# VectorE empties bank 7 (GEMM halves, spatial gating) ahead of the next units' maxima in the first block's attention

## The chip, the cores and the metric

The kernel runs on one core of one Trainium2 chip. The metric is the device time of one execution in microseconds. The engines are TensorE (PE, with its weight loads as PEld), VectorE (DVE), ScalarE (ACT), GpSimd (POOL) and SyncE (SP). Each runs its own list of instructions in order, and they meet through semaphores.

## The reference, cut to what matters

Two blocks follow each other. The first has two layers, each with a projection, a mixer and a feed-forward part; the change is in the mixer. Of that the parts below matter here: three attention branches over 512 positions and 8 heads, and a spatial gating that is computed beside them.

```python
def first_block(x, ...):
    for l in range(DEPTH):                      # DEPTH = 2
        h = rmsnorm(x, attn_norm[l])
        (q, kc, vc, ksl, vsl, kwn, vwn, gts, gq, gk, gv, ga, gr, uv) = split_columns(h @ w_in[l])
        o_nsa = nsa_mixer(q, kc, vc, ksl, vsl, kwn, vwn, gts, ...)
        o_gla = gla_mixer(gq, gk, gv, ga, gr, ...)
        o_sg = spatial_gating(uv, ...)
        x = x + jnp.concatenate([o_nsa, o_gla.astype(x.dtype), o_sg], axis=-1) @ w_out[l]
        ...
def spatial_gating(uv, ln_g, ln_b, w_s, b_s):
    u, v = jnp.split(jax.nn.gelu(uv), 2, axis=-1)
    v = layernorm(v, ln_g, ln_b).reshape(B, nch, SG_CHUNK, SG_GROUPS, SG_CH)
    s = jnp.einsum('gij,bnjgc->bnigc', jnp.tril(w_s), v) + b_s.T[None, None, :, :, None]
    out = u.reshape(B, nch, SG_CHUNK, SG_GROUPS, SG_CH) * s
...
        s = jnp.einsum('bqghd,bkgd->bghqk', qb, kwb)      # in nsa_mixer, per block of queries
        p = masked_softmax(s, wmask[None, None, None])
        o_win = jnp.einsum('bghqk,bkgd->bqghd', p.astype(vwb.dtype), vwb)
```

## The kernel before, in words

Positions lie along the free axis of most tiles, channels on the 128 partitions. A GEMM of the first block takes 24 products of 128x512 into one of eight PSUM banks: eight slices, each as three products of high and low parts (lines 454, 457, 458).

The attention of a layer is cut into 32 units. A unit u is one pair of heads j, one block of 128 queries, and one branch: even units are the selected branch (there are 8 blocks of keys and up to 16 may be selected, so every earlier block is), odd units the window branch. A loop over v = 0 to 15 handles two units per turn; step is v modulo 4, and j is v divided by 4. Every engine has this loop written out in its own order, and there is no scheduler.

- **TensorE**, turn v: turn(2v), the transposes of the probabilities of unit 2v (line 706); the scores of units 2v+2 and 2v+3 (line 690, four banks, 0 to 3); turn(2v+1); the value products of units 2v-1 and 2v (line 742); then one extra piece of work, which uses bank 7. At step 0 it is turn_compressed, the transposes of the compressed branch's probabilities (line 726). At step 1 it is the next compressed scores (line 716). At steps 2 and 3 it is half of a GEMM, by the table HALVES: su1 at v = 2 and 3, gr0 at 6 and 7, gr1 at 10 and 11. At v = 13 and 14 it is the spatial gating (line 789, by GATING_AT).
- **VectorE**, turn v: the maxima of units 2v+2 and 2v+3 (line 1842, four reductions of masked scores, each with a read of its accumulator); the emptying of bank 7 if the turn before ended a GEMM (evict_half, line 1924) or a gating (gated, line 1931); scale(2v+2), a reciprocal and two multiplications (lines 1882 and 1887); at some steps work of the compressed branch; scale(2v+3); at some turns statistics for the gating (gating_stats) or low parts for the output GEMM (out_low, line 1918).
- **ScalarE**, turn v: turned_copy(2v) out of banks 4 and 5 (line 1304), the exponentials of unit 2v+2 (line 1282), turned_copy(2v+1), the exponentials of unit 2v+3, and at step 0 the copy of turned compressed probabilities (line 1295).

So the maxima of a unit release its exponentials, those release scale, and scale releases turn on TensorE in the next turn. Whoever fills bank 7 next waits until VectorE has emptied it. With the table, a GEMM ends in bank 7 at v = 3, 7 and 11, is emptied at v = 4, 8 and 12, and what waits for the bank there is turn_compressed. The first gating is emptied at v = 14, and the second one waits for it.

Of the kernel before, what the change touches and what calls it, by code (L numbers as in the profile page):

```python
# [122 lines left out]
def row_block(u):  # L123

    i = u // 2 % NT
    return i if u % 2 == 0 else NT - 1 - i
# [25 lines left out]
def build(nc, a_x, a_w, a_cmp, a_mod, a_c, a_const, a_misc, a_vec, a_rgw, a_rpb, a_out):  # L152
# [8 lines left out]
    with ctx:  # L161
# [117 lines left out]
        def m_(name):  # L279
            return misc[:, MISC[name][0]:MISC[name][1]]  # L280
# [119 lines left out]
        def filling(name):  # L400
            b, k = uses[name]
            return full[b], k + 1

        def emptying(name):
            b, k = uses[name]
            return free[b], k + 1
# [5 lines left out]
        def emptied(name):  # L412
            return free[uses[name][0]]
# [1149 lines left out]
        def _(dve):  # L1563
# [74 lines left out]
            for l in range(DEPTH):  # L1638
# [187 lines left out]
                U = HEADS * NT  # L1826
# [7 lines left out]
                def maxima(u):  # L1834
                    i, br = row_block(u), u % 2
                    w = (i + 1) * P
                    for hh in range(2):
                        dve.wait_ge(*filling((l, "S", hh, u)))
                    s2 = PS[:, 2 * br:2 * br + 2, :]
                    mask = before_diag[:, S - w:S]  # L1840
                    for hh in range(2):
                        V.tensor_tensor_reduce(s2[:, hh, 0:w], s2[:, hh, 0:w], mask, -1.0, -2 * NEG_MASK, ALU.add, ALU.min,  # L1842
                                               nmax[:, br, hh:hh + 1]).then_inc(max_ok.sem, 1)
                        dve.wait_ge(max_ok.sem, max_ok.raised())

                def compressed_masked(j):
                    dve.wait_ge(*filling((l, "Sc", j)))
                    sc = PS[:, 7, 0:NT * 64].rearrange("p (n h c) -> p n h c", h=2, c=32)[:, :, :, 0:NC]
                    pc = Pc[:, :, :, 0:NC]
                    if j:  # L1850
                        dve.wait_ge(*filling((l, "PTc", j - 1)))
                    TT(pc, sc, cm.unsqueeze(2).to_broadcast([P, NT, 2, NC]), ALU.add).then_inc(emptied((l, "Sc", j)), 1)
                    dve.wait_ge(*emptying((l, "Sc", j)))

                def compressed_distances(j):
                    pc = Pc[:, :, :, 0:NC]
                    V.tensor_reduce(maxc[:, :, :], pc, AX.X, ALU.max).then_inc(dve_chain.sem, 1)
                    dve.wait_ge(dve_chain.sem, dve_chain.raised())
                    TT(pc, pc, maxc[:, :, :].unsqueeze(3).to_broadcast([P, NT, 2, NC]), ALU.subtract)\
                        .then_inc(maxc_ok.sem, 1)  # L1860
                    dve.wait_ge(maxc_ok.sem, maxc_ok.raised())

                def scale_compressed(j):
                    pc = Pc[:, :, :, 0:NC]
                    dve.wait_ge(expc_ok.sem, expc_ok.seen_by("dve"))
                    V.tensor_reduce(sumsc[:, :, :], pc, AX.X, ALU.add).then_inc(dve_chain.sem, 1)
                    dve.wait_ge(dve_chain.sem, dve_chain.raised())
                    V.reciprocal(rc[:, :, :], sumsc[:, :, :]).then_inc(dve_chain.sem, 1)
                    dve.wait_ge(dve_chain.sem, dve_chain.raised())
                    both = 2 * j * BR + 2  # L1870
                    TT(rc[:, :, :], rc[:, :, :], gN[:, :, both:both + BR + 1:BR], ALU.mult).then_inc(dve_chain.sem, 1)
                    dve.wait_ge(dve_chain.sem, dve_chain.raised())
                    TT(pc, pc, rc[:, :, :].unsqueeze(3).to_broadcast([P, NT, 2, NC]), ALU.mult).then_inc(scaledc.sem, 1)
                    dve.wait_ge(scaledc.sem, scaledc.raised())

                def scale(u):
                    j, i, br = u // (2 * NT), row_block(u), u % 2
                    w = (i + 1) * P
                    both = 2 * j * BR + br
                    for hh in range(2):  # L1880
                        dve.wait_ge(*emptying((l, "S", hh, u)))
                    V.reciprocal(r3[:, 0:2], sums[:, br, 0:2]).then_inc(dve_chain.sem, 1)
                    dve.wait_ge(dve_chain.sem, dve_chain.raised())
                    for hh in range(2):
                        pr = work[:, 2 * br + hh, 0:w]
                        gate = gN[:, i, both + BR * hh:both + BR * hh + 1]
                        TS(pr, pr, r3[:, hh:hh + 1], gate, ALU.mult, ALU.mult).then_inc(scaled.sem, 1)  # L1887
                        dve.wait_ge(scaled.sem, scaled.raised())
# [5 lines left out]
                def gating_stats(n):  # L1894

                    if n == 0:
                        dve.wait_ge(*emptying((l, "sv1", "T")))
                    V.bn_stats(small[:, 8 + 6 * n:14 + 6 * n], sv[:, :, n, :]).then_inc(dve_chain.sem, 1)
                    dve.wait_ge(dve_chain.sem, dve_chain.raised())
                    V.bn_aggr(small[:, 32 + 2 * n:34 + 2 * n], small[:, 8 + 6 * n:14 + 6 * n]).then_inc(dve_chain.sem, 1)  # L1900
                    dve.wait_ge(dve_chain.sem, dve_chain.raised())
                    if n == NT - 1:
                        TS(small[:, 44:48], small[:, 33:40:2], EPS, None, ALU.add).then_inc(dve_chain.sem, 1)
                        dve.wait_ge(dve_chain.sem, dve_chain.raised())
                        TS(small[:, 40:44].bitcast(U32), small[:, 44:48].bitcast(U32), 1, None, ALU.logical_shift_right)                            .then_inc(dve_chain.sem, 1)
                        dve.wait_ge(dve_chain.sem, dve_chain.raised())
                        V.reciprocal(small[:, 48:52], small[:, 40:44]).then_inc(gating_ok.sem, 1)
                        dve.wait_ge(gating_ok.sem, gating_ok.raised())
# [6 lines left out]
                def out_low(k):  # L1915

                    dve.wait_ge(h_hi.sem, h_hi.seen_by("dve"))
                    TT(o_lo[k], mixed[k], o_hi[k].bitcast(F32), ALU.subtract).then_inc(h_lo.sem, 1)
                    dve.wait_ge(h_lo.sem, h_lo.raised())

                def evict_half(name):

                    dve.wait_ge(*filling((l, name)))
                    TT(proj[:, T[name], :], PS[:, 7, :], rstd[:, :], ALU.mult).then_inc(emptied((l, name)), 1)
                    dve.wait_ge(*emptying((l, name)))

                def gated(t):

                    key = (l, "sg", t)
                    dve.wait_ge(*filling(key))  # L1930
                    TT(sq[:, t, :].rearrange("p (n c) -> p n c", c=P), PS[:, 7, :].rearrange("p (n c) -> p n c", c=P),
                       m_("sgb")[:, t * P:(t + 1) * P].unsqueeze(1).to_broadcast([P, NT, P]), ALU.add)\
                        .then_inc(emptied(key), 1)
                    dve.wait_ge(*emptying(key))
# [9 lines left out]
                scale(1)  # L1944
                for v in range(U // 2):
                    j, step = v // NT, v % NT
                    for u in (2 * v + 2, 2 * v + 3):
                        if u < U:
                            maxima(u)
                    if v - 1 in HALVES and HALVES[v - 1][1] == 1:  # L1950
                        evict_half(HALVES[v - 1][0])
                    if v - 1 in GATING_AT:
                        gated(GATING_AT.index(v - 1))
                    if 2 * v + 2 < U:
                        scale(2 * v + 2)
                    if step == 2 and j + 1 < HEADS // 2:
                        compressed_distances(j + 1)
                    elif step == 3 and j + 1 < HEADS // 2:
                        scale_compressed(j + 1)
                    if 2 * v + 3 < U:  # L1960
                        scale(2 * v + 3)
                    if v in STATS_AT:
                        gating_stats(STATS_AT.index(v))
                    if v in CONVERT_AT:
                        out_low(CONVERT_AT.index(v))
                    if step == 1 and j + 1 < HEADS // 2:
                        compressed_masked(j + 1)
# [650 lines left out]
```

## Time and profile before

| | before |
|---|---|
| median of 3 runs | 1894.14 us (1894.01 to 1894.18) |
| the profiled execution | 1893.17 us, its span 1890.5 us |
| TensorE busy | 1835.7 us, 97% |
| GpSimd busy | 1530.4 us, 81% |
| VectorE busy | 1121.3 us, 59% |
| ScalarE busy | 659.7 us, 35% |

The two attention loops lie near 155 to 260 us and 795 to 900 us of the span. Shares are means over the whole span; in a window of the first loop, 145 to 265 us, TensorE was busy for 105.96, VectorE for 101.42 and ScalarE for 82.08 of 120 us.

### The profile page before, as it was taken

The page shows a single profiled execution, that of the slowest core. Times are in us where ns is not written, and L with a number is a line of the kernel's source. Part 1 is how long each engine was busy: PE and PEld are TensorE (multiplying, and loading weights), DVE is VectorE, ACT ScalarE, POOL GpSimd, SP SyncE. Part 2 cuts the span into 40 slices and gives each one's busy share as a digit, 9 for nine tenths or more (in the row PEclk, how much of TensorE's full clock was granted, in tenths as well). Part 3 has the DMA queues.
Part 4 walks back from the last instruction along what each step waited for, and adds up shares of the span by engine and source line. Part 5 has one row for each costly group of instructions (what it writes and reads, how often), then busy time and mean ns, then how long its engine had stood idle before and what let it go on. Part 6 is the DMA issues. An engine that isn't in the chain of part 4 may idle for free.

```text
span 1890.5 us, 28094 instructions
## 1 busy us (share of the span) xinstructions
PE 1835.7 (97%) x10354; PEld 1463.3 (77%) x10354; DVE 1121.3 (59%) x1627; ACT 659.7 (35%) x1146; POOL 1530.4 (81%) x1093
## 2 busy tenths in 40 slices
PE   8998899999999999988999999999999999999997
PEld 6776678888888877766888888888877777778885
DVE  4778865574366456888546415767846667650342
ACT  4356652110011232767321001123556665640112
POOL 8993569988888898715998878988799998689994
PEclk9999999999999999999999999999999999999999
DMA  5251023443344223300234333532223333323231
GB/s 200 79 162 40 13 68 110 135 132 101 100 134 123 89 79 104 120 13 24 89 102 145 121 95 106 153 116 77 89 84 87 97 85 93 83 77 101 89 100 45
DMA packets 68690, 182.53 MB, mean 97 GB/s; under 512 B 23888, under 2 KB 24144, under 8 KB 68432
## 3 DMA queue, kind: packets, MB, share of 16 engines
q1 hardware_dynamic: 60480, 154.48, 26.3%
q10 hardware_dynamic: 8080, 26.32, 4.4%
q8 instruction: 82, 1.34, 0.3%
q14 instruction: 48, 0.39, 0.1%
HBM read 178.67 MB, written 2.10 MB: 96 GB/s over the span
## 4 chain that ended last, share of the span: by engine, by line
PE 78%; DVE 8%; POOL 6%; issue 4%; ACT 3%; DMA 0%; SPq 0%; POOLq 0%; DVEq 0%; ACTq 0%
PE PS L454 23%; PE PS L458 23%; PE PS L457 23%; POOL w_lo L2325 3%; DVE work L1887 2%; POOL w_hi L2320 2%; POOL w_hi L2318 1%; PE PS L997 1%; DVE PS L1842 1%; ACT work L1282 1%; PE PS L690 1%; PE PS L586 1%; PE PS L918 1%; PE PS L955 1%; ACT work L1304 1%
## 5 line engine op out<-in xcount | busy, mean ns | idle before, releaser
L2325 POOL TENSOR_TENSOR w_lo<-raw,w_hi 128x256 fp32r<-128x256 f32 (+2 forms) x606 | 786.3, 1297 | 64.9 <-ACT w_hi L1389 16.8
L454 PE MATMUL PS<-a_hi,w_hi 128*128 128x512 f32 x1168 | 462.8, 396 | 5.6 <-POOL w_lo L2325 5.0
L458 PE MATMUL PS<-a_hi,w_lo 128*128 128x512 f32 x1168 | 455.5, 390 | 0.0
L457 PE MATMUL PS<-a_lo,w_hi 128*128 128x512 f32 x1168 | 455.5, 390 | 0.0
L2318 POOL TENSOR_SCALAR w_hi<-raw 128x512 fp32r<-128x512 f32 x226 | 372.4, 1648 | 100.8 <-PE PS L454 84.7
L2320 POOL TENSOR_TENSOR w_hi<-raw,const 128x1024 fp32r<-128x1024 f32 (+1 forms) x192 | 339.6, 1769 | 100.9 <-PE PS L454 95.2
L454 PEld LDWEIGHTS PS<-a_hi,w_hi 128*128 128x128 f32 x1168 | 219.5, 188 | 62.2 <-issue 8.4
L458 PEld LDWEIGHTS PS<-a_hi,w_lo 128*128 128x128 f32 x1168 | 219.7, 188 | 46.7
L457 PEld LDWEIGHTS PS<-a_lo,w_hi 128*128 128x128 f32 x1168 | 219.8, 188 | 44.7 <-issue 0.7
L454 PE MATMUL PS<-b_hi,w_hi 128*128 128x512 f32 x552 | 222.1, 402 | 3.4 <-ACT zs L1462 2.9
L457 PE MATMUL PS<-b_lo,w_hi 128*128 128x512 f32 x552 | 215.2, 390 | 0.0
L458 PE MATMUL PS<-b_hi,w_lo 128*128 128x512 f32 x552 | 214.8, 389 | 0.0
L2003 DVE TENSOR_TENSOR work<-PS,rstd 128x512 f32<-128x512 f32 x88 | 60.9, 692 | 148.5 <-PE PS L458 143.2
L1376 ACT ACTIVATE work<-work 128x512 f32<-128x512 f32 x44 | 27.8, 633 | 313.4 <-DVE small L2007 313.3
L454 PE MATMUL PS<-f_hi,w_hi 128*128 128x512 f32 x352 | 136.9, 389 | 0.0
L457 PE MATMUL PS<-f_lo,w_hi 128*128 128x512 f32 x352 | 136.9, 389 | 0.0
L458 PE MATMUL PS<-f_hi,w_lo 128*128 128x512 f32 x352 | 136.9, 389 | 0.0
L454 PEld LDWEIGHTS PS<-b_hi,w_hi 128*128 128x128 f32 x552 | 103.5, 188 | 33.1 <-issue 7.4
L458 PEld LDWEIGHTS PS<-b_hi,w_lo 128*128 128x128 f32 x552 | 103.7, 188 | 22.0
L457 PEld LDWEIGHTS PS<-b_lo,w_hi 128*128 128x128 f32 x552 | 103.7, 188 | 22.0 <-issue 1.9
L2014 DVE TENSOR_TENSOR f_lo<-work,f_hi 128x512 fp32r<-128x512 f32 x44 | 85.5, 1944 | 36.5 <-ACT f_hi L1379 36.5
L2061 DVE TENSOR_TENSOR x<-PS,x 128x512 f32<-128x512 f32 x32 | 22.1, 692 | 139.4 <-PE PS L458 139.2
(343 smaller groups left out, 2687.4 us busy)
## 6 DMA issues: line engine op xcount, KB each, us to landing
raw<-weights SPq DMA_DIRECT2D x278, 512.0 KB, 3.5
work<-mod_w ACTq DMA_DIRECT2D x24, 512.0 KB, 3.5
work<-cmp_w ACTq DMA_DIRECT2D x4, 1024.0 KB, 7.2
proj<-cmp_w ACTq DMA_DIRECT2D x4, 1024.0 KB, 5.6
bias<-rpb SPq DMA_DIRECT2D x256, 12.0 KB
rgw<-rgw ACTq DMA_DIRECT2D x8, 256.0 KB, 2.7
out<-xc SPq DMA_DIRECT2D x8, 256.0 KB, 2.6
const<-const SPq DMA_DIRECT2D x1, 1436.5 KB, 15.1
```

Of the source, the lines that this page charges most:

```text
L454: ins = nc.tensor.matmul(out, wh, hi, start=start, stop=False)
L457: nc.tensor.matmul(out, wh, lo, start=False, stop=False)
L458: return nc.tensor.matmul(out, wl, hi, start=False, stop=stop)
L586: ins = nc.tensor.matmul(out, level[lv % 3][r, c], later_halves(level[lv % 3][r, c], half), start=True, stop=True, tile_position=(GDK * h, 0))
L1376: A(work[:, f % 2, :], work[:, f % 2, :], ACT.Silu).then_inc(to_dve.sem, 1)
L1887: TS(pr, pr, r3[:, hh:hh + 1], gate, ALU.mult, ALU.mult).then_inc(scaled.sem, 1)
L2003: TT(work[:, w0 + f % 2, :], PS[:, b0 + f % 2, :], rstd[:, :], ALU.mult)\
L2014: TT(f_lo[:, f, :], work[:, 4 + f % 2, :], f_hi[:, f, :].bitcast(F32), ALU.subtract)\
L2061: TT(x[:, m, :], PS[:, uses[key][0], :], x[:, m, :], ALU.add).then_inc(emptied(key), 1)
L2318: G.tensor_scalar(w_hi[:, r, k, :], raw[:, r, k, :], 1.0, None, ALU.mult).then_inc(pool_chain, 1)
L2320: G.tensor_tensor(w_hi[:, r, k, :], raw[:, r, k, :], ones[:, k, :], ALU.mult).then_inc(pool_chain, 1)
L2325: ins = G.tensor_tensor(w_lo[:, r, k, :], raw[:, r, k, :], w_hi[:, r, k, :].bitcast(F32), ALU.subtract)
```

## The change

On VectorE, the lines that empty bank 7 stand ahead of the maxima of the next two units instead of behind them.

```diff
                 for v in range(U // 2):
                     j, step = v // NT, v % NT
-                    for u in (2 * v + 2, 2 * v + 3):
-                        if u < U:
-                            maxima(u)
                     if v - 1 in HALVES and HALVES[v - 1][1] == 1:
                         evict_half(HALVES[v - 1][0])
                     if v - 1 in GATING_AT:
                         gated(GATING_AT.index(v - 1))
+                    for u in (2 * v + 2, 2 * v + 3):
+                        if u < U:
+                            maxima(u)
                     if 2 * v + 2 < U:
                         scale(2 * v + 2)
```

In VectorE's order at v = 4 of the first layer, where the GEMM su1 is emptied, the difference reads as follows. L1842 is a masked maximum over the scores of one head (256 columns wide for unit 10, 384 for unit 11; each stands twice, for two heads, and each is followed by the read of its accumulator), L1924 the eviction, L1882 and L1887 are scale(10).

```order
 L1900 BN_AGGR small<-small 128x2
-L1842 ISA PS,nmax<-PS,before_diag 128x256
-L1842 ISA nmax 128x1
...
-L1842 ISA PS,nmax<-PS,before_diag 128x384
...
 L1924 TENSOR_TENSOR proj<-PS,rstd 128x512
+L1842 ISA PS,nmax<-PS,before_diag 128x256
+L1842 ISA nmax 128x1
...
+L1842 ISA PS,nmax<-PS,before_diag 128x384
...
 L1882 RECIPROCAL r_92<-sums 128x2
 L1887 TENSOR_SCALAR work<-work,r_92,gN 128x256 x2
```

The eviction has passed the four maxima; scale(10) stays behind both. The same stands at v = 8 and 12 and in the second layer.

At v = 14 of the first layer it is the addition of the gating's bias out of bank 7 (L1931) that moves, past the maxima of units 30 (512 columns) and 31 (128 columns); L1918 is a low part for the output GEMM.

```order
 L1918 TENSOR_TENSOR proj_r<-proj,proj_r 128x512
-L1842 ISA PS,nmax<-PS,before_diag 128x512
...
-L1842 ISA PS,nmax<-PS,before_diag 128x128
...
 L1931 TENSOR_TENSOR sq<-PS,misc 128x512
+L1842 ISA PS,nmax<-PS,before_diag 128x512
...
+L1842 ISA PS,nmax<-PS,before_diag 128x128
...
 L1882 RECIPROCAL r_92<-sums 128x2
 L1887 TENSOR_SCALAR work<-work,r_92,gN 128x512 x2
```

Again only the one instruction has changed its place against the maxima. The orders of the other four engines are the same row for row.

## Rows read from the trace of the kernel before

**Rows 1.** The page: busy time of each engine; the chain that ended last.

```profile
PE 1835.7 (97%) x10354; PEld 1463.3 (77%) x10354; DVE 1121.3 (59%) x1627; ACT 659.7 (35%) x1146; POOL 1530.4 (81%) x1093
...
PE 78%; DVE 8%; POOL 6%; issue 4%; ACT 3%; DMA 0%; SPq 0%; POOLq 0%; DVEq 0%; ACTq 0%
```

**Rows 2.** Lines 1924 and 1931, and who waited for them (us, times).

```profile
L1924 DVE TENSOR_TENSOR proj<-PS,rstd x6: 691/691/691, 183.9 to 876.8; 128x512 f32<-128x512 f32 x6
...
  PE PS L726: 15.5, 6
...
L1931 DVE TENSOR_TENSOR sq<-PS,misc x4: 690/692/692, 248.4 to 893.3; 128x512 f32<-128x512 f32 x4
...
  PE PS L789: 3.2, 2
```

**Rows 3.** Timeline, VectorE, second layer, v = 4: start, us, idle before <- releaser.

```profile
822.20 0.43 DVE L1842 CUSTOM_DVE_ANT_0 PS<-PS,before_diag 128x256 f32<-128x256 f32 x1
...
824.56 0.69 DVE L1924 TENSOR_TENSOR proj<-PS,rstd 128x512 f32<-128x512 f32 x1
825.29 0.17 DVE L1882 RECIPROCAL r<-sums 128x2 f32<-128x2 f32 x1
...
826.54 0.17 DVE L1882 RECIPROCAL r<-sums 128x2 f32<-128x2 f32 x1 [0.18 <-ACT work L1282]
...
827.77 0.57 DVE L1842 CUSTOM_DVE_ANT_0 PS<-PS,before_diag 128x384 f32<-128x384 f32 x1
```

**Rows 4.** Timeline, ScalarE and TensorE, the same stretch.

```profile
822.78 0.47 ACT L1282 ACTIVATE work<-PS,nmax 128x256 f32<-128x256 f32 x1 [1.12 <-DVE nmax L1842]
...
823.97 1.02 ACT L1304 ACTIVATE work<-PS 128x1024 f32<-128x1024 f32 x1
...
825.40 0.60 PE L726 MATMUL PS<-const,Pc 128*64 128x128 f32 x4 [2.60 <-DVE proj L1924]
...
830.97 0.83 PE L706 MATMUL PS<-const,work 64*128 64x64 f32 x12 [0.18 <-DVE work L1887]
```

**Rows 5.** Timeline, TensorE, second layer, v = 0 to 1, behind line 726.

```profile
799.71 0.69 PE L706 MATMUL PS<-const,work 64*128 64x64 f32 x8 [1.39 <-DVE work L1887]
```

**Rows 6.** Timeline, VectorE and ScalarE, the other places of line 1924.

```profile
187.67 0.57 DVE L1842 CUSTOM_DVE_ANT_0 PS<-PS,before_diag 128x384 f32<-128x384 f32 x1 [0.60 <-PE PS L690]
...
213.37 0.57 DVE L1842 CUSTOM_DVE_ANT_0 PS<-PS,before_diag 128x384 f32<-128x384 f32 x1
...
237.70 0.17 DVE L1882 RECIPROCAL r<-sums 128x2 f32<-128x2 f32 x1
...
236.92 0.59 ACT L1295 ACTIVATE PTc<-PS 64x512 f32<-64x512 f32 x1
...
853.68 0.57 DVE L1842 CUSTOM_DVE_ANT_0 PS<-PS,before_diag 128x384 f32<-128x384 f32 x1 [0.75 <-PE PS L690]
...
880.75 0.57 DVE L1842 CUSTOM_DVE_ANT_0 PS<-PS,before_diag 128x384 f32<-128x384 f32 x1
...
883.20 0.81 ACT L1304 ACTIVATE work<-PS 128x768 f32<-128x768 f32 x1 [0.36 <-ACT work L1282]
```

**Rows 7.** Timeline, VectorE, ScalarE and TensorE, first layer, v = 14.

```profile
249.29 1.13 DVE L1887 TENSOR_SCALAR work<-work,r,gN 128x512 f32<-128x512 f32 x2
...
248.47 0.60 ACT L1304 ACTIVATE work<-PS 128x512 f32<-128x512 f32 x1
...
249.11 1.58 PE L789 MATMUL PS<-misc,proj 128*64 128x128 f32 x16 [1.59 <-DVE sq L1931]
250.63 0.71 PE L706 MATMUL PS<-const,work 64*128 64x64 f32 x16
```

**Rows 8.** Windows (PEclk is the granted clock) and two score products on TensorE.

```profile
852.00:853.00 1.00, 1.00 (x6) 0.65 (x6) 0.89 (x2) 0.82 (x2) 0.81 (x3) 0.50 0.00 0
...
826.59 1.30 PE L690 MATMUL PS<-keys,proj 64*128 64x384 f32 x8
...
851.87 2.44 PE L690 MATMUL PS<-keys,proj 64*128 64x384 f32 x8
```

## The prediction

> **What bounds the kernel now.** The first view to read is the page [rows 1]: TensorE is busy for 97% of the span and carries 78% of the chain that ended last. What TensorE waits for is therefore worth something, if what releases it really comes sooner. The second view is that of the two lines that the change moves [rows 2]. TensorE waited 15.5 us in all for line 1924, in six waits, and 3.2 us for line 1931, in two. These 18.7 us are what the change seems to offer. The third view is the timeline of one such place on all three engines [rows 3, 4], and it tells another story.
>
> Take the eviction of su1 in the second layer. VectorE starts the maxima of unit 10 at 822.20 with no idle time ahead of them (the row has no bracket), goes from maxima to eviction (824.56) to the reciprocal of unit 10 (825.29) without a gap, and TensorE's transposes of the compressed probabilities (line 726) wait 2.60 us, to 825.40 [rows 3, 4]. But the next thing in TensorE's order is turn(10), and that waits for scale(10), which is the next thing in VectorE's order behind the eviction. VectorE is the bound here. The same stretch where nothing is to be evicted shows it: at v = 0 of the second layer line 726 has no eviction to wait for, and TensorE then idles all the same, 1.39 us for line 1887, the multiplications of scale [rows 5].
>
> **The change part by part.** Nothing is added or removed. Eight evictions, three halves and one gating per layer, move ahead of four maxima and their accumulator reads; the second gating, at v = 15, has no maxima to pass. TensorE, ScalarE, GpSimd and SyncE keep their order, and no DMA moves.
>
> *What comes sooner.* Start to start the eviction takes 825.29 - 824.56 = 0.73 us [rows 3], and its four maxima 824.56 - 822.20 = 2.36 us. So bank 7 comes free 2.4 us earlier, and line 726 runs about that much earlier. The eviction itself finds its bank ready: TensorE issues the half GEMM ahead of the scores that the maxima read, and those were there (no bracket at 822.20). No new wait is charged.
>
> *What that is worth.* Scale(2v+2) starts behind the same work as before, evictions and maxima in the other order, so turn(2v+2) starts when it did. TensorE's idle time moves from ahead of line 726 to behind it. Value: nothing, at all six places of line 1924.
>
> *What comes later.* The maxima start 0.73 us later, and ScalarE had been idle, waiting for them: 1.12 us ahead of the first exponential [rows 4]. Behind that exponential ScalarE goes on almost without a break (the copy of turned unit 9 at 823.97, then the exponentials of unit 11), and VectorE's reciprocal for unit 11 waits for it, 0.18 us, at 826.54 [rows 3]. Scale(10) has room: the exponentials of unit 10 end by 823.97, so at 824.70 after the change, ahead of 825.29. Scale(11) has none. It starts 0.73 us later, and the maxima of unit 12 at 827.77, which followed without a gap, start 0.73 us later too. TensorE waits next for VectorE's line 1887 at 830.97 already (0.18 us) [rows 4], so it passes the delay on, into the half GEMMs behind it and so to the end of the attention.
>
> The price at each place is 0.73 us less whatever idle time follows:
> - First layer, v = 4: VectorE waits 0.60 us for scores at 187.67 [rows 6]; 0.73 - 0.60 = 0.13 is left.
> - First layer, v = 8: the maxima at 213.37 follow without a gap; 0.73.
> - First layer, v = 12: scale(27) starts at 237.70 with no wait, and ScalarE had been through its exponentials since 236.92 [rows 6], a room of 0.78; 0.
> - Second layer, v = 4: 0.73, as above.
> - Second layer, v = 8: a wait of 0.75 at 853.68 [rows 6] takes it; 0.
> - Second layer, v = 12: the maxima at 880.75 follow without a gap, but ScalarE has 0.36 us of idle ahead of the next copy, at 883.20 [rows 6] (the page names ScalarE's own work as its releaser; by the code the copy waits for TensorE's value products as well); 0.73 - 0.36, so about 0.4.
>
> *The gating, v = 14, twice.* Here TensorE's own work is held: the second gating starts at 249.11 after 1.59 us of waiting, and turn(30) follows right behind it at 250.63, while scale(30) multiplies from 249.29 to 250.42 [rows 7]. After the change the gating runs in the idle time. Turn(30) is then held by scale(30) alone, whose exponentials end 0.73 us later (248.47 + 0.73 = 249.20; with about 0.1 for the signal and 0.2 for the reciprocal the multiplications run 249.5 to 250.6). But half of the 16 transposes of turn(30) need only the first multiplication and go ahead of 250.6. They took 0.71 us in all from 250.63; with half of them out of the way turn(30) ends some 0.2 us earlier. I take a gain of 0.2 us in each layer. Its bounds are 0 (scale(30) holds it as late as before) and 1.59 (the whole wait).
>
> The sum: 0.13 + 0.73 + 0 - 0.2 in the first layer, 0.73 + 0 + 0.4 - 0.2 in the second, together +1.6 us. Against the profiled execution, 1893.17 us, that is 1894.8. The median, 1894.14, lies 0.97 us above it, so **1895.7 us**.
>
> *TensorE's clock.* At four of the six places of line 1924, and at v = 0 of the second layer, the granted clock falls to half behind TensorE's idle time: 0.50 in 852 to 853 us [rows 8], which is the 1.2 GHz level. The eight score products of 384 columns and fewer then took 2.44 us at 851.87 against 1.30 at 826.59 [rows 8], so a fall costs about 1.1 us at most, part of it beside VectorE's work. The waits of 0.60 and 0.75 us for scores that absorb the delay above stand in such stretches. The change leaves TensorE's work the same and moves 0.6 us of it (line 726) from the end of the idle time to its start. I count no fall more and none less. The bounds are two falls more (the two places that have none now, +2.2) and all four gone (-4.4).
>
> The Trainium skill ("TensorE: Matmul & The Clock Gate", Part 1, What's actually happening) says that half rate is the default and activity releases it, and that where the change falls depends on a phase that runs free of the kernel; this trace agrees that the fall follows idle time at most of the places and not at all. By that rule moving line 726 could shift falls either way, which is the third rival.
>
> **The rivals.** First, the 18.7 us are given back: 1894.1 - 18.7 = 1875.4. For it speaks only the table of waits; against it the gapless VectorE rows and the idle time at v = 0. Chance 4%. Second, nothing passes on, neither loss nor gain, 1894.1, if idle time that I have not followed absorbs the late scale: 12%. Third, the clock keeps its full level at the four places that have a fall now: 1.6 - 4.4 = -2.8, so 1891.3 at best, since the waits of 0.60 and 0.75 us that absorb delay would go too. Chance 6%. Fourth, on the slow side: the late exponentials are absorbed nowhere, at the gatings neither. The place is ScalarE between the maxima and scale(2v+3); the price 0.73 at each of eight, +5.8 us, so 1900.0. It decides the sign by my measure from six places on (6 x 0.73 = 4.4). For it speaks that ScalarE waits for maxima at every place; against it the waits of 0.60 and 0.75 and the room of 0.78. Chance 10%.
>
> **How the numbers follow.** My forecast has the remaining 68%. A measurement of this kernel can tell about 0.2%, that is 3.8 us, from no change. The forecast lies inside that, as do the second rival and most of the third; the first (4%) and what of the third goes beyond its price (2%) are faster, 6%; the fourth and the forecast with two falls more (1.6 + 2.2 = 3.8, on the bound) (1%) give slower, 11%; the same is left with 83%. The range of 1892.4 to 1898.3 takes in one fall fewer with the losses half absorbed at the low end, and two falls more or most of the fourth rival at the high end.
>
> **What would show it.** In the changed trace line 726 should start within 0.2 us of the value products or of the eviction, whichever ends last, and the wait for line 1924 should all but vanish; a wait of 2 us and more should stand ahead of line 706 instead, released by line 1887. ScalarE's idle time ahead of the first exponential should be 0.7 longer at these places, and scale(2v+3) 0.7 later against the start of the iteration at the first layer's v = 8 and the second's v = 4. The second gating should start about 1.5 us earlier. The prediction is wrong if TensorE's total idle time in the two attentions falls by several us, or if the eviction at its new place waits for the half GEMM.

## The result and the profile after

The changed kernel takes 1901.24 us (median of 18 runs, 1896.33 to 1906.54), the kernel before beside it 1894.60 us (1892.73 to 1899.31): a ratio of 1.0034, 95% interval 1.0025 to 1.0043. It is slower by 6.6 us, beyond the 0.2% that this kernel's measurement can tell, and above the top of the forecast range, 1898.3. The profiled execution of the changed kernel took 1902.52 us, so its trace stands for the middle of its runs. That of the kernel before, 1893.17 us, is among its fastest, with a granted clock of 0.992, where the 80 runs of that kernel beside the experiments below have a median of 0.990. So the two traces differ by 9.4 us and not by 6.6, and a comparison of them shows too much rather than too little of what the clock does.

The page of the changed kernel answers to [rows 1], and the view of lines 1924 and 1931 to [rows 2].

```profile
PE 1847.1 (97%) x10354; PEld 1473.1 (78%) x10354; DVE 1116.9 (59%) x1627; ACT 659.7 (35%) x1146; POOL 1532.7 (81%) x1093
...
PE 78%; DVE 8%; POOL 6%; issue 4%; ACT 3%; DMA 0%; SPq 0%; POOLq 0%; DVEq 0%; ACTq 0%
```

```profile
L1924 DVE TENSOR_TENSOR proj<-PS,rstd x6: 690/691/692, 181.7 to 881.4; 128x512 f32<-128x512 f32 x6
...
  PE PS L726: 1.5, 4
...
L1931 DVE TENSOR_TENSOR sq<-PS,misc x4: 691/691/692, 249.3 to 901.8; 128x512 f32<-128x512 f32 x4
```

The waits went: 15.5 us for line 1924 became 1.5, and the 3.2 for line 1931 became none. Yet TensorE is busy for 1847.1 us instead of 1835.7, with the same 10354 instructions. They got longer. The timeline of the second layer at v = 4 (start, us, idle before and its releaser) shows the rest; it answers to [rows 3, 4].

```profile
827.95 0.69 DVE L1924 TENSOR_TENSOR proj<-PS,rstd 128x512 f32<-128x512 f32 x1
828.67 0.43 DVE L1842 CUSTOM_DVE_ANT_0 PS<-PS,before_diag 128x256 f32<-128x256 f32 x1
...
831.04 0.17 DVE L1882 RECIPROCAL r<-sums 128x2 f32<-128x2 f32 x1
...
833.01 0.17 DVE L1882 RECIPROCAL r<-sums 128x2 f32<-128x2 f32 x1 [0.91 <-ACT work L1282]
...
834.24 0.57 DVE L1842 CUSTOM_DVE_ANT_0 PS<-PS,before_diag 128x384 f32<-128x384 f32 x1
...
829.26 0.47 ACT L1282 ACTIVATE work<-PS,nmax 128x256 f32<-128x256 f32 x1 [1.85 <-DVE nmax L1842]
...
828.79 0.60 PE L726 MATMUL PS<-const,Pc 128*64 128x128 f32 x4 [0.23 <-DVE proj L1924]
831.80 0.84 PE L706 MATMUL PS<-const,work 64*128 64x64 f32 x8 [2.42 <-DVE work L1887]
832.43 2.45 PE L690 MATMUL PS<-keys,proj 64*128 64x384 f32 x8
```

Line 726 starts 0.23 us behind the value products, and TensorE then idles 2.42 us for line 1887: the wait moved behind line 726. ScalarE waits 1.85 us for its first maximum instead of 1.12, and the reciprocal of unit 11 waits 0.91 instead of 0.18: both 0.73 more, what the eviction takes start to start. All that was forecast. But the score products at 832.43 take 2.45 us, where they took 1.30 at this place before [rows 8].

The windows of the two attentions (after the length: busy time of PE, PEld, DVE, ACT, POOL, then the granted clock) say why. First the changed kernel, with the head of the first layer's output GEMM between the two, then the kernel before.

```profile
145.00:265.00 120.00, 107.36 (x994) 79.95 (x994) 98.44 (x279) 81.47 (x190) 46.61 (x60) 0.89 0.08 25
254.00:263.00 9.00, 8.52 (x49) 6.47 (x50) 5.56 (x9) 8.68 (x11) 2.86 (x3) 0.62 0.00 1
785.00:910.00 125.00, 111.28 (x1038) 83.10 (x1035) 103.26 (x287) 82.94 (x194) 52.46 (x65) 0.95 0.09 27
```

```profile
145.00:265.00 120.00, 105.96 (x1022) 78.97 (x1023) 101.42 (x283) 82.08 (x191) 49.80 (x61) 0.97 0.10 32
254.00:259.00 5.00, 5.00 (x31) 3.61 (x25) 3.05 (x4) 4.85 (x6) 3.89 (x3) 1.00 0.00 0
785.00:910.00 125.00, 111.70 (x1041) 83.31 (x1041) 102.31 (x284) 83.34 (x193) 55.03 (x64) 0.96 0.10 31
```

A stretch of 120 us at a mean clock of 0.89 holds 2 x 0.11 x 120 = 26 us at half clock; before it was 7. With the second layer (12 against 10) that is 39 against 17 us. One place stands out, 254 to 263 us: a mean of 0.62, so some 7 us at half clock, at full clock before. There the output GEMM starts, and TensorE is the bound. TensorE's rows ahead of it, in the first layer at v = 13 to 15, answer to [rows 7]; below them those of the kernel before.

```profile
245.51 1.53 PE L789 MATMUL PS<-misc,proj 128*64 128x128 f32 x16
...
250.66 1.53 PE L789 MATMUL PS<-misc,proj 128*64 128x128 f32 x16
253.48 0.95 PE L706 MATMUL PS<-const,work 64*128 64x64 f32 x16 [1.29 <-DVE work L1887]
...
256.25 2.83 PE L742 MATMUL PS<-work,proj 128*64 128x128 f32 x24
259.00 0.80 PE L454 MATMUL PS<-proj_r,w_hi 128*128 128x512 f32 x1
...
264.42 0.39 PE L458 MATMUL PS<-proj_r,w_lo 128*128 128x512 f32 x1
```

```profile
242.21 1.53 PE L789 MATMUL PS<-misc,proj 128*64 128x128 f32 x16
...
252.81 1.53 PE L742 MATMUL PS<-work,proj 128*64 128x128 f32 x24
254.27 0.50 PE L454 MATMUL PS<-proj_r,w_hi 128*128 128x512 f32 x1
...
258.30 0.39 PE L458 MATMUL PS<-proj_r,w_lo 128*128 128x512 f32 x1
```

The second gating joins the value products ahead of it, and the idle time of 1.29 us stands behind it, close to the next idle time ahead of turn(31). The value products behind take 2.83 us, where the same 24 took 1.53 us in the kernel before. From the start of the first gating to that of the 18th product of the output GEMM it is 264.42 - 245.51 = 18.91 us, before 258.30 - 242.21 = 16.09: this place costs 2.8 us. In the second layer the output GEMM keeps its full clock, and the same stretch takes 15.71 us, before 16.05.

The 18 runs of the changed kernel carry their granted clocks, and the time goes with them: the four at 0.990 took 1896.33 to 1898.58 us, the five at 0.986 took 1900.86 to 1904.07, the two at 0.982 took 1906.41 and 1906.54. At one and the same clock the two kernels lie closer: those four at 0.990 have a median of 1897.2 us; 24 of the 80 runs of the kernel before have 0.990 too, and their median is 1894.8. By this estimate some 2.4 of the 6.6 us do not go with the mean clock, and the other 4 do.

### The profile page after: what moved, and what is told of

It is laid out like the page before. It is cut to its first block, busy times and chain, and to the rows that moved or that the text cites. A ratio compares the mean times of both kernels' runs of the same rounds, so it can differ in the third digit from the quotient of the medians.

```text
span 1900.1 us, 28094 instructions
## 1 busy us (share of the span) xinstructions
PE 1847.1 (97%) x10354; PEld 1473.1 (78%) x10354; DVE 1116.9 (59%) x1627; ACT 659.7 (35%) x1146; POOL 1532.7 (81%) x1093
## 4 chain that ended last, share of the span: by engine, by line
PE 78%; DVE 8%; POOL 6%; issue 4%; ACT 3%; DMA 0%; SPq 0%; POOLq 0%; DVEq 0%; ACTq 0%
PE PS L454 23%; PE PS L458 23%; PE PS L457 23%; POOL w_lo L2325 3%; DVE work L1887 2%; POOL w_hi L2320 2%; PE PS L997 1%; POOL w_hi L2318 1%; ACT work L1282 1%; DVE PS L1842 1%; ACT work L1304 1%; PE PS L918 1%; PE PS L586 1%; PE PS L955 1%; PE PS L742 1%
```

## The experiments

Two theories; the code cuts are shortened. **A**: the clock. The free bank lets TensorE do its leftover work at once, so its idle time lies unbroken behind it and the clock falls more often. **B**: the late exponentials, 0.73 us per place, as the prediction had them.

**One half of the change at a time.** The first kernel moves only the evictions, the second only the gating.

```diff
 evict_half(...)          # e1: ahead        e2: behind maxima
 for u in (2 * v + 2, 2 * v + 3): maxima(u)
 gated(...)               # e1: behind       e2: ahead of maxima
```

> Only the evictions of the GEMM halves (line 1924) stand ahead of the maxima; the gatings stay behind them. Theory A (clock): with bank 7 free early, TensorE's leftover work is done at once and the idle time behind it is unbroken, so the granted clock falls more often. In the traces the half-clock time of the two attentions went from 17 us to 41 us, and the worst of it, 7 us at the head of the output GEMM of the first layer, stands behind the second gating, which this kernel leaves alone. A expects more half-clock time than the 17 us of before, some 25 to 33 us, and 2 to 4 us over the kernel before. Theory B (late exponentials): ScalarE starts 0.73 us late at six places and nothing else matters; B expects the forecast's terms, about +2.0 us, with as much half-clock time as before.

Measured: 1898.79 us, ratio 1.0019 (1.0010 to 1.0028), +4.0 us on its medians. In its profiled execution the two attentions have mean clocks of 0.96 and 0.95, some 22 us at half clock: under the 25 to 33 that A expected, and not far over the 17 of before. Over its 11 runs the granted clock has a median of 0.988. Its six runs at 0.988 have a median of 1899.0 us, seven of the kernel before at that clock 1897.1, so about 2 of the 4 us are no matter of the mean clock; that part is what B expected.

> Only the gating at v = 14 (line 1931) moves ahead of the maxima; the halves stay behind them. A (clock): the second gating joins TensorE's work ahead of it, the idle time between it and turn(30) gets unbroken, and the output GEMM, which is bound by TensorE, starts at half clock in part of the executions; +2 to +4 us over before. B (late exponentials): the forecast's term, 0.2 us faster in each layer, -0.4 us.

Measured: 1899.77 us (1893.76 to 1906.84), ratio 1.0026 (1.0012 to 1.0041). The gating alone, one instruction per layer for which I had forecast a gain of 0.2 us, costs 5 us, and spreads the runs over 13 us: five of the 11 (1893.76 to 1896.72) are as fast as the kernel before, and the other six, from 1899.77 up, have granted clocks of 0.987 and less. In its profiled execution, one of the slow ones (1904.11 us), the head of the output GEMM has the clock that the changed kernel showed:

```profile
252.00:261.00 9.00, 8.67 (x53) 6.35 (x50) 5.47 (x10) 8.75 (x12) 2.80 (x2) 0.62 0.00 1
```

The output GEMM of the second layer begins at half clock too, and from the first gating to the 18th product the two layers take 18.83 and 18.80 us, 2.7 us over before in each. B falls as the only cause. The two halves together give 9.0 us, more than the change; with an interval of 2.3 to 7.8 us for the gating alone that does not show that they fail to add.

This run also warns of sums of half-clock time in single executions. It runs the halves as the kernel before does, and its attentions still have mean clocks of 0.90 and 0.92, some 44 us at half clock, no less than the 39 of the changed kernel.

**TensorE held where it stood.** VectorE's order is that of the change.

```diff
+if j: pe.wait_ge(max_ok.sem, 2 * U * l + 2 * (2 * NT * j + 4))     # turn_compressed
+if t == 1: pe.wait_ge(max_ok.sem, 2 * U * (l + 1))                 # second gating
```

> The changed kernel, but TensorE is held: at v = 4, 8 and 12 it starts the transposes of the compressed probabilities, and at v = 14 the second gating, only when VectorE has done the last maximum of the turn. VectorE's order stays that of the change and its exponentials stay 0.73 us late; TensorE's idle time stands again ahead of line 726, as in the kernel before. A (clock): half-clock time goes back toward the 17 us of before, and the time to +1 to +3 us over before. B (late exponentials): nothing changes against the changed kernel, +6.6 us.

Measured: 1895.35 us, ratio 1.0004 (0.9995 to 1.0013): no difference from before. With TensorE's idle time back ahead of line 726, the late exponentials cost 0.8 us (-0.9 to +2.5 by the interval). The granted clock of its runs has a median of 0.990, as before. Its profiled execution, 1894.95 us, has as many long falls at the halves as the changed kernel (a mean clock of 0.93 and 0.95 in the two windows) and none at the output GEMM. So a fall's price depends on its place, and at the output GEMM it is higher.

> Only the gating at v = 14 ahead of the maxima, and TensorE starts the second gating only behind the last maximum of the turn, so its idle time stands ahead of it as in the kernel before; the exponentials of units 30 and 31 are 0.73 us late. A (clock): the 5 us that the gating alone cost come from the idle time that got unbroken behind the early gating, so they go: 0 to +1 us over before. B (late exponentials at the gating): as without the hold, +5 us.

The edit is the second of the two waits above, in the kernel that moves the gating alone. Measured: 1895.88 us, ratio 1.0003 (0.9994 to 1.0012). The 5 us of the gating are gone. Its exponentials are late as before, so they cost nothing that can be measured; where TensorE's idle time stands does.

**Idle time filled.** Repeating work into the same place leaves the result as it is.

```diff
-for i in range(NT):                                   # turn_compressed
+for i in list(range(NT)) * (5 if j else 1):
-for hh in range(2):                                   # spatial_gating
+for hh in list(range(2)) * (2 if t else 1):
```

> The changed kernel, but TensorE fills its idle time with work that changes nothing: at v = 4, 8 and 12 it does the four transposes of the compressed probabilities five times instead of once (four more at about 0.43 us each, 1.7 us of an idle time of 2.4), and the second gating twice, each time into the same places of bank 7. A (clock): the granted clock stays up at these places, half-clock time of the two attentions falls to 10 us or less, and the time goes to 0 to 4 us below the kernel before. B (late exponentials): TensorE waits anyway, so the time stays at +6.6 us over before or goes above it.

Measured: 1895.53 us, ratio 1.0003 (0.9994 to 1.0012). The 6.6 us are back, but nothing below the kernel before. In its profiled execution both output GEMMs still begin at half clock (a mean of 0.81 in 254 to 263 us).

That completes a count. Three profiled executions have the early gating without a hold: the changed kernel, the gating alone, and this one. Of their six output GEMMs five begin at half clock. Of the 18 in the nine other executions, the kernel before and the runs below included, none does.

> Only the halves' evictions ahead of the maxima (the gatings behind, as before), with the transposes of the compressed probabilities five times at v = 4, 8 and 12 and four times at v = 0. The exponentials are 0.73 us late at six places. A (clock): against the run with the halves only (+4.0 us over before) the falls at these places go away, and the time is 1 us above to 2 us below the kernel before. B (late exponentials): the repeats change nothing, +4.0 us over before.

Measured: 1895.13 us, ratio 0.9999 (0.9990 to 1.0009), at a mean clock of 0.997 over the whole span (0.992 before). That lies in the range A gave, but a full clock should be worth something against the kernel before, and here it is not: something eats it.

**The eviction between the two maxima**, alone and with repeats.

```diff
+maxima(2 * v + 2)
 evict_half(...); gated(...)
-for u in (2 * v + 2, 2 * v + 3): maxima(u)
+maxima(2 * v + 3)
-for i in range(NT):                                   # e6 only
+for i in list(range(NT)) * (3 if j else 4):
```

> The eviction (or the gating's addition) stands between the maxima of the two units: behind those of unit 2v+2 and ahead of those of unit 2v+3. ScalarE's first exponentials are then on time, and the second ones have a copy of about 1.0 us ahead of them, so none is late. B (late exponentials) expects the time of the kernel before, within 1 us. A (clock): line 726 runs about 1.3 us earlier than before, in the middle of TensorE's idle time instead of at its end or its start, and the second gating 0.8 us earlier with almost no idle time behind it; as many falls as before at the halves, none more at the output GEMM, and the time within 1.5 us of before.

Measured: 1894.84 us, ratio 0.9996 (0.9987 to 1.0005). Both theories expected that. In its profiled execution the attentions have mean clocks of 0.91 and 0.96, some 31 us at half clock, and none of it at the output GEMMs.

> The eviction between the two units' maxima, as in the run before this one, and TensorE repeats the four transposes of the compressed probabilities, three times in all at v = 4, 8 and 12 and four times at v = 0, into the same places, so that the result is the same. A (clock): granted clock up at nearly all of these places, half-clock time in the two attentions under 8 us, and a time 2 to 4 us below the kernel before: faster than both kernels. B (late exponentials): no exponential is late and TensorE only fills idle time, so the time of the kernel before, within 1 us.

Measured: **1887.15 us** (1886.92 to 1888.45), ratio 0.9958 (0.9944 to 0.9971): faster than both kernels, by twice what A expected, and with the narrowest spread of all. Its granted clock is 1.00 in both attentions.

**What eats the gain.** The next kernel is this fast one with one thing changed: the evictions stand ahead of both maxima.

> The fast kernel of the runs so far (eviction between the two units' maxima, line 726 repeated, 7.5 us under before) with one thing changed: the evictions of the halves stand ahead of both units' maxima, as in the change; the gating stays between, the repeats stay. So the clock stays up and the exponentials of the even units come 0.73 us late at six places, with no wait for scores at half clock behind them to absorb it. B (late exponentials cost at full clock): +4.4 us over the fast kernel (6 x 0.73), up to +7 if VectorE's multiplications also run into GpSimd's weight splitting at v = 12; so 0.5 to 3 us under before. A (clock alone counts): the same time as the fast kernel, 7.5 us under before.

Measured: 1894.47 us, ratio 0.9992 (0.9983 to 1.0001), so 0.34% or 6.4 us over the fast kernel at the same clock. That is B's number, not A's: at full clock the late exponentials, with what follows from them, cost nearly the whole gain. VectorE's rows of the second layer show the two parts. First the kernel with the evictions ahead, at v = 4, 11 and 12; below it the fast kernel.

```profile
826.86 0.17 DVE L1882 RECIPROCAL r<-sums 128x2 f32<-128x2 f32 x1 [0.91 <-ACT work L1282]
...
869.15 1.56 DVE L1887 TENSOR_SCALAR work<-work,r,gN 128x128 f32<-128x128 f32 x2
...
872.72 1.96 DVE L1887 TENSOR_SCALAR work<-work,r,gN 128x512 f32<-128x512 f32 x2
...
878.01 0.86 DVE L1887 TENSOR_SCALAR work<-work,r,gN 128x256 f32<-128x256 f32 x2
```

```profile
823.23 0.17 DVE L1882 RECIPROCAL r<-sums 128x2 f32<-128x2 f32 x1 [0.19 <-ACT work L1282]
...
864.88 0.73 DVE L1887 TENSOR_SCALAR work<-work,r,gN 128x128 f32<-128x128 f32 x2
...
867.60 1.38 DVE L1887 TENSOR_SCALAR work<-work,r,gN 128x512 f32<-128x512 f32 x2
...
872.31 1.69 DVE L1887 TENSOR_SCALAR work<-work,r,gN 128x256 f32<-128x256 f32 x2
```

The reciprocal waits 0.91 us instead of 0.19, 0.72 more; six times that is 4.3 us. And in both layers two multiplications at v = 11, which run while GpSimd splits weights, take longer: 1.56 and 1.96 us instead of 0.73 and 1.38, another 1.4 us, of which 0.8 come back at v = 12, where those of unit 26 take 0.86 instead of 1.69. Together that is 4.3 + 2 x 0.6 = 5.5 us, and the two profiled executions lie 5.6 us apart (1894.01 and 1888.45). The delay is not all that decides between the long and the short pair: the second layer of the kernel before has the long one (1.57 and 1.95 us), and so has the first layer with the gating alone moved (1.40 and 2.19).

> The kernel before with the repeats alone: line 726 three times at v = 4, 8 and 12, four times at v = 0; VectorE's order is that of before, so bank 7 comes free at the end of TensorE's idle time and the repeats (0.87 us at each of six places) stand ahead of turn(2v+2). A (clock): the idle time ahead of them is unbroken as before, so the falls at v = 4, 8 and 12 stay in part, and the repeats delay turn(2v+2) by up to 0.87 us: 0 to +5 us over before. If repeats alone were what makes the fast kernel fast, it would be some 5 to 7 us under before.

Measured: 1899.45 us, ratio 1.0026 (1.0017 to 1.0035). The repeats alone make it slower; the bank must come free early for them to lie in idle time.

## Why the prediction was wrong

- *The offered 18.7 us are no gain.* Right. The waits vanished, TensorE waits for line 1887 instead, and nothing came sooner.
- *The price of late exponentials, 0.73 us less what follows.* Right by place in the traces. From the first maxima of v = 3 to those of v = 5 the second layer took 827.77 - 815.49 = 12.28 us before and 834.24 - 821.24 = 13.00 after, 0.72 more, and the kernel with TensorE held, which has the late exponentials and little else, stands at +0.8 where I had summed 1.6 with the gating's gain. At the same granted clock the changed kernel stands at +2.4. That idle time at half clock absorbs part of it fits too: where the clock stays up, the price rises to 6.4 us. The sum left out one term, VectorE's multiplications while GpSimd splits weights: at v = 11 of the first layer they take 1.42 and 2.18 us in the changed kernel, 0.73 and 1.38 before. As the gating alone has the long ones there too, the change need not be what brings them.
- *The gating, a gain of 0.2 us per layer.* Wrong. It is a loss of about 5 us in all, by its effect on the clock; the hold takes it away whole. Where the clock stays at 0.990 and more, the kernel with the gating alone takes 1893.76 to 1896.15 us, neither gain nor loss that could be told.
- *The clock: "I count no fall more and none less", bounds of 1.1 us a fall.* **This is the step that failed.** The granted clock of the runs fell from a median of 0.990 to 0.986, and half clock came to a place that had none, the output GEMM, where TensorE is the bound. There some 7 us at half clock cost 2.8 us, two and a half times my price, which took the eight score products for the whole of a fall. And the place was not on my list: I had listed the six places of line 1924 and v = 0, not what follows the gating. With both holds the clock is back at 0.990, and 6.6 - 0.8 = 5.8 us are gone.
- *The rivals.* The fourth, slow, had the sign and nearly the size (+5.8), but by a mechanism (late exponentials absorbed nowhere) that the holds show to be worth 0.8 us here. The third was about the clock, which decided, but I gave it only the fast sign and 6%. The Trainium skill ("TensorE: Matmul & The Clock Gate", Part 1, What's actually happening) says that half rate is the default, that activity releases it, and that the phase of this runs free of the kernel. The runs agree in that the granted clock differs from run to run of one kernel, 0.982 to 0.990 in the changed one. That moved work can therefore shift falls either way was my conclusion from it, and it should have had a slow side.

Left open: how often the clock falls at each place over many executions, since each kernel has one profile. That the early gating lowers the clock at the output GEMM is shown, by five of six output GEMMs against none of 18 and by the hold. At the halves it is not shown by the traces, as the gating alone has as much half clock there; only the runs speak for it, with a median clock of 0.988 and +4.0 us, of which about 2 stand at equal clock. Why the clock answers to the new order is not shown either: TensorE's idle time is no longer than before (2.42 us against 2.60 at v = 4 of the second layer, 1.29 against 1.59 at the gating), it stands behind the moved work instead of ahead of it. And of the 9.4 us between the two traces 1.6 arise at 1671 to 1676 us, behind both attentions, in code that the change leaves alone: a mean clock of 0.66 in the changed kernel, 1.00 at that place before.

## What to carry to other kernels

A wait that is removed from an engine that is released by the next instruction of the same producer anyway only moves its idle time; look at what the engine waits for next before counting it. Where idle time moves on TensorE, ask what runs behind it at half clock, above all whether a stretch follows that TensorE bounds. And put an instruction that frees a resource where neither the chain of the next consumer nor the one behind it starts with it: between the two maxima it delays nothing, and the freed bank can then take harmless repeats that hold the clock up, worth 0.4% here.

## What the runs showed of the hardware that I had not expected

The same program spread over 10 us from run to run (1896.33 to 1906.54), with granted clocks from 0.990 down to 0.982, and the kernel whose idle time is filled over 1.5 us in five runs (1886.92 to 1888.45). Repeated transposes, 0.87 us of them at six places and 1.3 us at v = 0 of the two layers, changed the kernel with the eviction between the maxima by 7.7 us (1894.84 to 1887.15), a quarter of the some 31 us at half clock in the attentions that they took away; at the output GEMM some 7 us at half clock cost 2.8. VectorE's two multiplications from SBUF to SBUF took 1.56 us in one run and 0.73 in another, at the same place of the program, while GpSimd split weights.

The Trainium skill ("SBUF — State Buffer", Who interferes with whom) says that such an operation can hold the port pair that VectorE and GpSimd share, and that the one who comes second waits for the other's whole instruction; the lengthened rows agree: the two end at 869.88 and 870.71 us, each 0.1 us behind the end of a GpSimd instruction (869.80 and 870.62). The short pair does not fit as well: it ran from 864.88 to 865.61, inside a GpSimd instruction of the same splitting (864.49 to 866.07, as far as the profile's rough spans of GpSimd tell). No run here takes GpSimd's work away to test it.
